# Experts of a two-layer network: tokens of two experts picked in one feature-major step, and eight kept weight units in place of six

## What is computed

```python
logits = xf @ w_router + b_router
top_v, top_i = lax.top_k(logits, TOP_K)
gates = softmax(top_v)
def expert_block(xb, e):
    g = xb @ w_gate[e] + b_gate[e]
    u = xb @ w_up[e] + b_up[e]
    g = minimum(g, 7.0); u = clip(u, -7.0, 7.0)
    glu = g * sigmoid(1.702 * g)
    return ((u + 1.0) * glu) @ w_down[e] + b_down[e]
y_rows = y_rows * row_gate[:, None]
out = segment_sum(y_rows, row_tok)[:T]
```

## Time and profile before

| what | before |
|---|---|
| median of 3 runs (lowest, highest) | 1994.51 us (1993.8, 1994.73) |
| span of the profiled execution | 1993.2 us |
| TensorE busy in the span | 1971.0 us (99%) |
| VectorE, ScalarE busy | 849.3 us, 421.3 us |
| read from HBM | 559.12 MB |
| first matmul of expert 0 | 190.92 us |
| last `select_T` of expert 31 | 1122.79 us |

### The profile page before, as it was taken

One profiled execution on the slowest core, in us unless ns is written; L12 is line 12 of the kernel. 1 busy time (PEld: TensorE's weight loads), 2 busy tenths in 40 slices (PEclk: granted clock), 3 DMA queues, 4 the chain that ended last, 5 costly groups with the idle time before them and its releaser, 6 DMA issues.

```text
span 1993.2 us, 29626 instructions
## 1 busy us (share of the span) xinstructions
PE 1971.0 (99%) x11290; PEld 1281.7 (64%) x11291; DVE 849.3 (43%) x1801; ACT 421.3 (21%) x827; POOL 22.6 (1%) x56
## 2 busy tenths in 40 slices
PE   9999999999999999999999999999999999999999
PEld 7676333333443344333333587889999886989999
DVE  5644212112121111121121358456766697557774
ACT  4442212112111121121122222231100122331100
POOL 0000000000000000000000020000000000000000
PEclk9999999999999999999999999999999999999999
DMA  9276999999999999999999943424445533334430
GB/s 360 86 268 273 404 422 422 419 421 422 422 405 408 421 421 389 423 422 419 420 421 423 421 175 135 185 100 144 168 169 188 190 127 127 136 118 149 170 132 19
DMA packets 81916, 565.21 MB, mean 284 GB/s; under 512 B 10208, under 2 KB 10880, under 8 KB 14240
## 3 DMA queue, kind: packets, MB, share of 16 engines
q1 hardware_dynamic: 80016, 556.92, 70.0%
q0 software_dynamic: 1808, 6.98, 0.9%
HBM read 559.12 MB, written 4.19 MB: 283 GB/s over the span
## 4 chain that ended last, share of the span: by engine, by line
PE 88%; DMA 8%; issue 1%; ACT 1%; POOL 0%; DVE 0%; ACTq 0%; SPq 0%; DVEq 0%; POOLq 0%
PE bank L677 22%; PE bank L1129 17%; PE bank L628 13%; PE bank L1148 9%; DMA ring<-in_stream 7%; PE bank L1069 3%; PE bank L1051 3%; PE bank L728 3%; PE bank L1172 3%; PE bank L836 3%; PE bank L1114 2%; PE bank L1202 1%; PE bank L1060 1%; DMA B<-B 1%; PE bank L1426 1%
## 5 line engine op out<-in xcount | busy, mean ns | idle before, releaser
L1129 PE MATMUL bank<-ring,sq 128*64 128x512 f32 x1888 | 415.6, 595 | 8.3 <-DMA ring<-in_stream 7.4
L1129 PEld LDWEIGHTS bank<-ring,sq 128*64 128x64 f32 x1888 | 132.0, 137 | 271.1 <-issue 245.0
L1636 ACT ACTIVATE B<-bank 128x256 f32<-128x256 f32 (+1 forms) x206 | 87.8, 456 | 658.8 <-PE bank L677 335.4
L1148 PE MATMUL bank<-ring,sq 128*64 128x512 f32 x896 | 198.4, 595 | 0.0
L628 PE MATMUL bank<-xn,ring 128*128 128x256 f32 x864 | 191.7, 382 | 0.3
L2603 DVE TENSOR_TENSOR xg<-bank,mbias 128x512 f32<-128x512 f32 x32 | 22.1, 692 | 375.4 <-PE bank L1114 330.8
L628 PEld LDWEIGHTS bank<-xn,ring 128*128 128x128 f32 x864 | 164.5, 191 | 25.8 <-issue 3.4
L677 PE MATMUL bank<-B,ring 128*128 128x128 f32 x1280 | 167.9, 275 | 0.0
L677 PEld LDWEIGHTS bank<-B,ring 128*128 128x128 f32 x1280 | 155.2, 192 | 0.0
L1148 PEld LDWEIGHTS bank<-ring,sq 128*64 128x64 f32 x896 | 61.8, 137 | 116.6 <-issue 116.3
L2583 DVE TENSOR_SCALAR B<-B 128x128 f32<-128x128 f32 x66 | 16.0, 283 | 261.9 <-PE bank L1040 261.9
(11 more groups left out here) (443 smaller groups left out, 2280.8 us busy)
## 6 DMA issues: line engine op xcount, KB each, us to landing
ring<-in_stream SPq DMA_DIRECT2D x513, 1024.0 KB, 13.8
B<-in_stream SPq DMA_DIRECT2D x6, 1024.0 KB, 10.5
mem_kv<-ring POOLq DMA_DIRECT2D x2, 1024.0 KB, 6.9
xT<-in_stream SPq DMA_DIRECT2D x2, 1024.0 KB, 10.3
B<-mem_kv POOLq DMA_DIRECT2D x2, 1024.0 KB, 7.2
xT<-in_x SPq DMA_DIRECT2D x4, 256.0 KB, 5.2
ring<-in_stream SPq DMA_DIRECT2D x4, 256.0 KB, 5.7
ring<-in_mem SPq DMA_DIRECT2D x1, 1024.0 KB, 10.7
```

Of the source, the lines that this page charges most:

```text
L1129: mm = pe.matmul(PS[4 + kind][NARROW * h:NARROW * (h + 1), :], xs[:, k % 4, NARROW * (k // 4):NARROW * (k // 4 + 1)], weights(e, j, kk, h) ...
L1148: mm = pe.matmul(PS[6][NARROW * h:NARROW * (h + 1), :], hT[0][:, f % 4, NARROW * (f // 4):NARROW * (f // 4 + 1)], weights(e, j, kk, h), st ...
L1636: return act.activation(out_, in_, fn, **kw)
```

## The change

1. **Picking.** `pick_tokens` and `turn_tokens` go out of the narrow pass. `pick_pair` makes the tokens of the two experts of the next pair at once and feature-major: the token matrix is the stationary operand, the selection matrix of the pair `psel` (two times 64 columns) the moving one, in eight products of 128 by 128 for half of the features. The first expert of a pair does one half, the second the other. Nothing has to be transposed; ScalarE copies each half once, and the first half once more at the end of the pair (`xs_next`). VectorE makes `psel` in four compares per pair (`select_pair`). In the wide pass the upper 64 tokens are still picked token-major (`pick_upper`, `turn_upper`).
2. **Loops.** Loops run over pairs of experts, with two experts in each loop's body; the expert next to a kept one stands outside the loops on TensorE.
3. **Kept units.** `KEPT_UNITS` are 4 to 11. Unit 5 goes to table space, unit 4 in four pieces to buffers of the norms. For expert 6 unit 5 is loaded with the others ahead of the experts, and unit 4 once the gate of expert 0 is through, ahead of turn 2. `RELOAD` is 8, not 10, so that the reload starts with turn 8, and ahead of it SP waits for the end of expert 6 as before.
4. **Tables.** `cos2` to `sin3` (0.5 MB) and `far`, `rcount` (0.3 MB) are loaded after turn 32, when all the experts' units have been issued, and VectorE waits for them ahead of the rotary step.

```diff
-RELOAD = 10 * E // 32
+RELOAD = 8 * E // 32
-KEPT_UNITS = (6, 7, 8, 9, 10, 11)
+KEPT_UNITS = (4, 5, 6, 7, 8, 9, 10, 11)
...
-                10: (flat4(prob), flat4(pT)), 11: (flat(tsq), flat(tv)), 6: (flat(xT),)}
+                10: (flat4(prob), flat4(pT)), 11: (flat(tsq), flat(tv)), 6: (flat(xT),),
+                5: (tab[:, TAT["cos1"]:TAT["cos1"] + 3 * 512], tb("far")),
+                4: (flat(un), std[:, :], rinv[:, :], reg(8192, 512))}
...
-            load_table("cos2", "sin3", S["router_loaded"])
-            load_table("before", "rcount", S["router_loaded"])
+            load_table("before", "iota", S["router_loaded"])
...
+            sp.wait_ge(S["qn_ready"], 3)
+            keep(KEPT[0], 5)
             sp.wait_ge(S["k_spilled"], 16)
...
+            sp.wait_ge(M["g_mm"], 1)
+            keep(KEPT[0], 4)
             turns_of(2, KEPT[0])
             turns_kept(KEPT[0])
-            turns_of(KEPT[0] + 2, RELOAD)
+            assert RELOAD == KEPT[0] + 2
             sp.wait_ge(S["units_done"], AT["moe"] + 12 * (KEPT[0] + 1))
...
-            turns_of(KEPT[1] + 2, turns)
+            turns_of(KEPT[1] + 2, E + 1)
+            load_table("cos2", "sin3", S["consts_loaded"])
+            load_table("far", "rcount", S["consts_loaded"])
+            turns_of(E + 1, turns)
...
-            def pick_tokens(n, w):
-
-                pe.wait_ge(M["sel_ready"], n + 1)
+            def pick_pair(half, bank):
+
+                for k in range(4 * half, 4 * half + 4):
+                    for tk in range(2):
+                        mm = pe.matmul(PS[bank][:, (k % 4) * P:(k % 4 + 1) * P], xtok[:, tk, k * P:(k + 1) * P],
+                                       psel[:, tk, :], start=(tk == 0), stop=(tk == 1))
+                mm.then_inc(M["xa_mm"], 1)
...
                 turn(n, 0, 0)
                 scatter_halves(n, 0)
                 turn(n, 0, 1)
-                pick_tokens(n + 1, 0)
+                pe.wait_ge(M["sel_ready"], pair_ready(p + 1, False))
+                pick_pair(r, 4)
                 scatter_halves(n, 1)
-                turn_tokens(n + 1, 0)
                 pe.wait_ge(M["h_ready"], nth(n, 0))
...
-                turn_tokens(n + 1, 0)
+                pe.wait_ge(M["sel_ready"], pair_ready(p + 1, general))
+                pick_pair(r, 5)
                 pe.wait_ge(M["selT_ready"], n + 2)
...
+            def copy_pair(n, r, bank, general):
+
+                act.wait_ge(M["xa_mm"], n + (5 if general else 3))
+                if r == 0:
+                    f(xs_next[:, :, :], of_bank(bank), ACT.Copy).then_inc(M["xs_ready"], 1)
+                else:
+                    f(xs[:, 4:8, :], of_bank(bank), ACT.Copy)
+                    f(xs[:, 0:4, :], xs_next[:, :, :], ACT.Copy).then_inc(M["xs_ready"], 1)
...
+            def select_pair(columns):
+
+                for r, (e, b) in enumerate(columns):
+                    io = tb("iota")[:, b * WIDE:b * WIDE + NARROW]
+                    for tk in range(2):
+                        last = ts(psel[:, tk, NARROW * r:NARROW * (r + 1)], io, key[:, tk, bass.ds(e, 1)], None,
+                                  ALU.is_equal)
+                last.then_inc(M["sel_ready"], 1)
...
             dve.wait_ge(S["un_ready"], UNSCALED[2] + 2)
+            dve.wait_ge(S["consts_loaded"], 80)
```

More of the change, by code:

```diff
@@ L436, in nth, with pair_ready, sel_ready @@
             return 2 * n + (w + 1)
+        def pair_ready(p, general):
+            return 3 * p + (1 if general else 0)
+        def sel_ready(p, r, general):
+            return 3 * p + (2 + 2 * r) + (1 if general else 0)
         block = ctx.enter_context(nc.Block())
@@ L1087, in weights @@
             def weights(e, j, kk, h):
-                if isinstance(e, int) and j in kept:
+                if isinstance(e, int) and e in KEPT and j in kept:
                     at = D * kk + 512 * h
-                    part = UNIT // len(kept[j])
-                    return kept[j][at // part][:, at % part:at % part + 512]
+                    for part in kept[j]:
+                        if at < part.shape[-1]:
+                            return part[:, at:at + 512]
+                        at -= part.shape[-1]
                 return ring[:, expert_slot(j), D * kk + 512 * h:D * kk + 512 * (h + 1)]
@@ L1258, in kept_expert, with experts_by_pairs @@
                 pe.br(f"pe_kept{e}_done")
                 pe.bass.switch_bb(f"pe_kept{e}_done", parent=here)
-                return e, here
+                return p, r, here
+            def experts_by_pairs():
+                slots = {pe.engine: LOOP_SLOT}
+                places = []
+                at = 0
+                for e in KEPT + (E,):
+                    with pe.bass.Fori(at, e // 2, engines=[pe.engine], head_slot=slots) as p:
+                        expert(p, 0)
+                        expert(p, 1)
+                    if e < E:
+                        for r in range(2):
+                            if r == e % 2:
+                                places.append(kept_expert(e // 2, r))
+                            else:
+                                expert(e // 2, r)
+                    at = e // 2 + 1
+                return places
@@ L1287, in _ @@
             pe.bass.switch_bb("pe_common", parent=entry)
-            kept_from = experts(expert, kept_expert)
+            kept_from = experts_by_pairs()
             pe.wait_ge(M["y_ready"], E + 1)
@@ L1945, in _ @@
             with act.If(most > WIDE):
+                copy_first_pair(2)
                 with act.Fori(0, E) as e:
                     for b in range(BLOCKS):
-                        act_pass(e * BLOCKS + b, True)
+                        act_pass(e * BLOCKS + b, b, True, True)
             with act.Else():
-                with act.Fori(0, E) as e:
-                    with act.If(act.value_load(load[0:1, bass.ds(e, 1)], min_val=0, max_val=T) < NARROW + 1):
-                        act_pass(e, False)
-                    with act.Else():
-                        act_pass(e, True)
-                    act.nop()
+                with act.Fori(0, E // 2) as p:
+                    for r in range(2):
+                        e = 2 * p + r
+                        with act.If(act.value_load(load[0:1, bass.ds(e, 1)], min_val=0, max_val=T) < NARROW + 1):
+                            act_pass(e, r, False)
+                        with act.Else():
+                            act_pass(e, r, True)
+                        act.nop()
             for i, j in enumerate(pair_order(2)):
@@ L2617, in swiglu, with dve_pass @@
                 return gate, product
-            def dve_pass(n, e, nb, ne, wide, general, chain_at, chain2_at):
+            def dve_pass(p, r, e, nb, ne, wide, general, chain_at, chain2_at):
+                n = 2 * p + r
                 step = Chain(dve, M["chain"], chain_at)
                 step2 = Chain(dve, M["chain2"], chain2_at)
-                dve.wait_ge(M["xa_mm"], 2 * n + 2)
+                dve.wait_ge(M["xs_mm"], nth(n, 0))
                 dve.wait_ge(M["selg_ready"], n + 1)
+                if r == 0:
+                    select_pair([(p + 1, b) for b in range(BLOCKS)] if general else
+                                [(2 * p + (2 + i), 0) for i in range(2)])
                 select(n + 1, ne, nb, general, step)
@@ L2658, in _ @@
             with dve.If(most > WIDE):
+                dve.wait_ge(M["xs_ready"], 1)
+                select_pair([(0, b) for b in range(BLOCKS)])
                 with dve.Fori(0, E) as e:
```

174 lines of the change are left out of this document (93 added, 81 removed).

## The result

The change makes the kernel slower: 2005.35 us (2002.64 to 2007.03) against 1994.15 us (1993.69 to 1994.73), a ratio of 1.0051 with a 95% interval of 1.0039 to 1.0064. The prediction said 1993.4 us with 0.11 for slower, and its range ended at 1998.3. The profiled execution has a span of 2003.2 us, 10.0 us more than before.

A forecast was written before the change was run, and what follows sets the result against it. The loads were taken to bound the experts' stage. Ledger -1.9, last expert's middle part -0.5, start +0.4 and tables +0.9 gave -1.1 us, from 1994.5 to 1993.4 us, no measurable change; range 1989.3 to 1998.3 us.

The forecast's parts named there:

- What bounds the kernel: Experts' stage: it ends when the loads are through, at the DMA engines' pace of 2.49 us a unit.
- TensorE's part: Narrow passes 0.53 us shorter each, 16 us over 30 experts; wide passes 0.67 us shorter, perhaps 0.4 more.
- The ledger: DMA bytes and empty time from expert 1's first load to expert 31's last up unit: -1.9 us in sum.
- The wait ahead of turn 8: First reload waits for the end of expert 6, engines stand still: +2.5 us, bounds +1.2 and +4.
- Thin queues behind kept experts: After experts 6 and 25, eight marks leave 5 us less queued: +1.0 us each, +2.0 in all.
- The window behind expert 18: 760 to 800 us: queue 2.7 us deeper, half of a 3.8 us loss regained, -1.9 us (bounds 0 and -3.8).
- The gap behind expert 0: 212 to 218 us, 270 GB/s: unit 4 is issued there and fills it, -1.5 us (bounds 0 and -2.2).
- Rival 3: Doubled loop bodies are fetched again in each pass: +3 to +10 us, 2000 us; chance 0.04.
- Start and tables: Ahead of the first matmul a later flag, +0.4 us; tables behind the experts' units delay the row swaps, +0.9 us.
- Rival 2: Row swaps behind the experts fall behind the ring's full queue: +4.1 us, 1998.6 us; chance 0.07.
- Rival 1: Loads find their slack in the experts' stage: -8.6 us, 1985.9 us, or 1990 with half; chance 0.19.
- rival 4: Loads are not the bound and TensorE's 16 us come through: 1979 us; chance 0.03.

The follow-up runs named there:

- pick_bare: pick_only with TensorE's wide pass left out of every expert that never takes it in this case; 1991.26 us, 0.9981 of the kernel before.
- kept_only: The kernel before with eight kept units, reload from turn 8 and late tables, but old picking and loops; 2002.92 us, 1.0042 of the kernel before.
- reload8: The kernel before with six kept units and only the reload moved, from turn 10 to turn 8; 1998.92 us, 1.0020 of the kernel before.
- after_bare: The changed kernel with TensorE's wide pass left out of every expert that never takes it in this case; 1997.36 us, 1.0015 of the kernel before.
- reload_mix: The kernel before with its six reloaded units put behind turns 13, 14, 15, 19, 20 and 21; 1994.04 us, 0.9996 of the kernel before.
- reload13: The kernel before with its six units reloaded from turn 13, one an expert; 1996.09 us, 1.0011 of the kernel before.
- pick_only: The changed kernel with six kept units, reload from turn 10 and early tables, so only picking and pair loops are new; 1997.40 us, 1.0007 of the kernel before.
- pick_slots: pick_only with its code shifted within blocks of 256 instructions, nothing else changed; 1996.97 us, 1.0015 of the kernel before.
- wide_away: The changed kernel with every wide pass of TensorE moved out of line, behind the stage's program; 2008.26 us, 1.0064 of the kernel before.
- pick_away: pick_only with every wide pass of TensorE moved out of line, behind the stage's program; 2006.88 us, 1.0060 of the kernel before.

## Why the prediction was wrong

- **What bounds the kernel: right.** The waits of 0.55 us at the end of expert 31 are still there, and all 17 kernels follow bytes plus idle time. TensorE's faster passes gave little of their own: *pick_bare* has all of them, some 16 us, without the gaps, and gained 0.19%, 3.5 us by the medians; in its profiled execution the stage ends 1.0 us sooner.
- **TensorE's part: right where nothing waits**, 0.57 for 0.53 us per narrow pass. The 0.15 us to pass `h_ready` on is what the kernel after shows: at expert 3 the product ends at 291.58 and the down matrix starts at 291.72 us, 0.14 us later; and the four compares of a pair, put at 0.8 us, take 0.74 (at 190.40 us). A wide pass with the narrow one behind it came down from 82.1 to 81.7 us, where 1.2 us less was forecast; a wait of 1.18 us for VectorE at the wide pass's down product, seen in all kernels with the new picking, stands in the way.
- **The ledger: the step that failed.** From the start of expert 1's loads to the last waiting units, the kernel before moved 380 MB in 912 us and the kernel after 380 MB in 924 (417 and 411 GB/s over 196 to 1108 and 196 to 1120 us). Figures rounded to 1 GB/s resolve some 2 us here, so these don't test the 2.5 us of bytes; the means of the table above agree with them. The idle time, put at +0.6 (-1.5 + 2.5 - 0.5 - 1.9 + 2.0), measured +13.0. By place: +6.3 us in 340 to 400, +8.1 in 900 to 1000, -1.5 in 520 to 640, -0.2 in 700 to 850.
  - *The wait ahead of turn 8*: +2.5 forecast, bounds 1.2 and 4; the window 380 to 390 loses 4.7 us, in *kept_only* 5.2, and 1.9 with six marks in *reload8*. The working had the units 0 to 7 of expert 7 queued in one piece behind unit 3 of expert 6; in fact they were issued one at a time from 358.91 us on, behind a queue that the marks had let run low, so all of them were through at some 380 us (358.91 + 1.1 + 8 x 2.49).
  - *Thin queues behind kept experts*: +1.0 each, by no row. Measured in *kept_only* 3.2 us in 350 to 380 (before 0.4) and 3.1 in 930 to 970 (before 0.4); in the kernel after 2.2 and 8.6, as the gap at 939.67 falls into the latter. In *kept_only* each lies within the bound "0 to 3.8 of a wide expert", but near three times the +1.0 taken; in the kernel after the second lies beyond it, since the forecast had no gap there.
  - *The window behind expert 18*: -1.9 forecast, -0.1 measured (382 GB/s, before 381). *pick_bare* and *after_bare* have 392 and 394 there, so about half of the gain comes where TensorE has no gaps. The place of the reloads isn't the reason: turn 20 has one behind expert 18 in the kernel before and after alike. *reload8*, which lost 2.4 us there, has none.
  - *The gap behind expert 0*: 298 for 270 GB/s, -0.4 in place of -1.5, and not even that is unit 4's doing. The test kernels with six units, which load nothing of the kind there, have 288 to 350 GB/s in the same window (*reload_mix* 288, *reload13* and *pick_bare* 298, *reload8* 309, *pick_only* 350).
- **The code's layout: not in the sum.** Rival 3 looked at instruction fetch, but for each turn of a loop; the turns run free, as the sum assumed. What came was a cost at the first jump over each wide pass, which no term or rival of the prediction had: 15.4 us of gaps, and three stretches at a granted clock of 0.50 behind them. By the medians of the bare kernels they cost 6 us in *pick_only* and use up what the picking gains; in the change they cost 8. The prediction looked at instruction packets only in the steady loops, one from 410 to 500 us, and for later turns that holds: *pick_only* has no packet on the queue q8 of instruction packets from 475 to 912 us. It says nothing of the first pass, and there the gaps are, which move with the position of the code in *pick_slots* (3.6 to 4.0 us ahead of 2, 8, 10 and 28).
- **Start and tables: sign wrong, size small.** +0.4 was forecast for the start, and the first gate begins 0.6 us sooner (190.31, before 190.92); in other kernels with the new picking it is at 189.3 to 191.5, so that is chance. For the tables +0.9 was forecast, -1.6 measured for all that is behind the experts; but this stretch is 868.8 to 871.8 us in the kernels with late tables and 868.9 to 872.0 in those with early ones, so neither a cost nor a gain of the tables is shown. Rival 2 falls: the second swap took 1.9 us more, and none of it reached the end.
- **Rival 1** falls with the ledger, rival 4 with the waits at expert 31.

What was only argued: that the gaps are fetches. In the kernel after a packet of 16 KB begins on the queue of instruction packets at 216.8, 408.8, 440.7, 936.0 and 995.0 us, within half a microsecond of the start of each of the five long gaps. It takes 1.0 to 1.2 us, less than any of them. And the kernel before has such a packet at 409.1 us, also at the end of expert 7, and no gap. DMA queues from 408 to 413 us, the kernel before and then the kernel after:

```profile
q8 instruction: 1, 0.02, 1.3%
...
q8 instruction: 1, 0.02, 1.3%
```

So such a packet alone cost the kernel before nothing. Why the kernel before, which also jumps over its wide pass, has no gap is open. Its jump lands at the end of the loop's body, next to the branch back to code already run, but so does the jump of a pair's second expert, and in *pick_slots* it is just these that have gaps of 3.6 to 4.0 us, ahead of 2, 10 and 28.

## What to carry to other kernels

Where the loads set the end, account for the time in which the DMA engines have nothing queued, and go through it place by place: here a run of skipped slots (191 GB/s in *kept_only*, 358 to 360 us), a load held for a release (32 GB/s in the kernel after, 382 to 384 us) and a stop of the consumer behind skipped slots (10 GB/s, 940 to 946 us) each let the queue run low or empty. Keeping data on chip saved its bytes (2.5 us by the means of the table) but took out what was queued at that place (the engines lost 3.2 us at expert 6 and 3.1 at expert 25 in *kept_only*); look at the depth that is left there, and at what lies between it and the next wait. When a loop body grows or is copied, jumps over code that is hardly ever taken can begin to cost, 15.4 us in all in the kernel after where the kernel before had none: look in the profile for idle time of TensorE without a releaser at the first turn.

## What the runs showed of the hardware

- A forward jump over a wide pass that TensorE makes for the first time cost up to 4.0 us (*pick_slots*, ahead of expert 28), depending on where the code lies, and in the kernel before nothing; entry into an out-of-line pass cost 5.9 to 6.2 us in three of four cases (*wide_away*, *pick_away*). Later turns of the same loop cost nothing that the trace shows: in the kernel after TensorE has, between 471.82 and 939.67 us, no idle time without a releaser but 0.40 and 0.36 us, both inside a wide pass (L1078 at 527.54 and 716.63 us).
- In the kernel after, behind idle stretches of TensorE of 3.78 us (413.02) and 2.17 (443.27), the products ran at half speed for some 3 us (granted clock 0.50 from 413 to 416 and from 444 to 446; at 443.27 3.49 us for eight in place of 1.94) and cost some 1.6 us more than the gap itself; behind that of 3.50 us (939.67) for some 5.5 us, granted clock 0.50 from 939 to 945, and 2.8 us more. Behind those of 2.33 us ahead of expert 1 and 2.27 ahead of 27 it did not happen (granted clock 1.00 from 219 to 225 and from 997 to 1003), nor behind the stops of 0.55 us at expert 31.
- Eight places of a ring of twelve that carry only a tiny load of 16x16 let the queue run low where six did not: with eight marks (*kept_only*) the engines fell to 191 GB/s in a window (358 to 360 us) in which six marks (the kernel before) left them at 418.
